# Hybrid attention and MoE step: the sums over values ahead of the turning back and of the second head's transposes

## What is computed

```
z = rmsnorm(x, g1) @ W_in                        # q, k, v of both mixers
s = q @ k.T * d**-0.5 (+ bias);  s = where(valid, s, -1e30)
p = softmax(s)  (mixer A: with a sink in the sum)
o = p @ v                                        # per head
x = x + concat(rmsnorm(oA), rmsnorm(oB)) @ W_out
x = x + sum over 2 chosen experts of w_e * (silu(h Wg) * (h Wu)) @ Wd,   h = rmsnorm(x, g2)
```

## Time and profile before

| | |
|---|---|
| runs before | 1029.91, 1031.77, 1031.78 us; median 1031.77 |
| profiled execution | 1031.24 us, span 1029.3 us, mean granted clock 0.982 |
| TensorE (PE) busy | 956.7 us, 93% of the span |
| VectorE (DVE) busy | 407.1 us, 40% |
| ScalarE (ACT) busy | 306.4 us, 30% |
| attention loop | about 303 to 671 us |
| the 16 DMA engines | about 0.9 busy in most slices behind the loop |

### The profile page before, as it was taken

One profiled execution on the slowest core, in us unless ns is written; L12 is line 12 of the kernel. 1 busy time (PEld: TensorE's weight loads), 2 busy tenths in 40 slices (PEclk: granted clock), 3 DMA queues, 4 the chain that ended last, 5 costly groups with the idle time before them and its releaser, 6 DMA issues. The chain is left out here.

```text
span 1029.3 us, 16232 instructions
## 1 busy us (share of the span) xinstructions
PE 956.7 (93%) x6079; PEld 489.7 (48%) x6079; DVE 407.1 (40%) x1246; ACT 306.4 (30%) x921; POOL 89.2 (9%) x72
## 2 busy tenths in 40 slices
PE   6999999999988989989898998898999999998995
PEld 3444554545365454555555565568444333333331
DVE  0342333422467465665746556575331111101110
ACT  1221222212346354554636445411111111111110
POOL 1000000000030000000000000001222222212111
PEclk9999999999989989999999989999999999999998
DMA  9500111001263011010101041188299999999972
GB/s 357 210 33 9 41 41 41 17 24 41 91 236 130 18 45 62 1 62 1 63 1 62 28 158 62 42 361 334 91 346 382 375 379 393 391 388 391 375 273 41
DMA packets 34441, 164.65 MB, mean 160 GB/s; under 512 B 7809, under 2 KB 9889, under 8 KB 20929
## 3 DMA queue, kind: packets, MB, share of 16 engines
q1 hardware_dynamic: 24192, 134.92, 33.0%
q0 software_dynamic: 6912, 17.32, 6.8%
q10 hardware_dynamic: 3264, 11.44, 2.8%
HBM read 147.10 MB, written 24.41 MB: 167 GB/s over the span
## 5 line engine op out<-in xcount | busy, mean ns | idle before, releaser
L1325 PE MATMUL ps<-arena 128*128 128x512 f32 (+1 forms) x640 | 251.2, 552 | 9.0 <-DMA arena<-in_w_in 9.0
L1325 PEld LDWEIGHTS ps<-arena 128*128 128x128 f32 x640 | 121.0, 190 | 134.1 <-issue 128.8
L1630 PE MATMUL ps<-arena 128*32 128x512 f32 x1536 | 173.8, 603 | 7.4 <-DMA arena<-in_wexp 6.6
L774 ACT ACTIVATE arena<-arena 128x256 f32<-128x256 f32 (+6 forms) x144 | 83.9, 583 | 129.5 <-DVE arena L1071 129.4
L1523 PE MATMUL ps<-arena 128*128 128x512 f32 x224 | 106.0, 605 | 0.0
L1630 PEld LDWEIGHTS ps<-arena 128*32 128x32 f32 x1536 | 51.5, 111 | 111.8 <-issue 107.9
L1067 DVE CUSTOM_DVE_ANT_0 arena<-ps,arena 128x256 f32<-128x256 f32 (+6 forms) x144 | 78.1, 542 | 31.8 <-PE ps L1412 31.5
L1648 PE MATMUL ps<-arena 128*32 128x512 f32 x768 | 87.3, 592 | 0.6 <-ACT arena L878 0.6
L1261 DVE SCALAR_TENSOR_TENSOR arena<-ps,arena 128x256 f32<-128x256 f32 x24 | 11.6, 484 | 167.4 <-ACT arena L870 167.4
L1427 PE MATMUL ps<-arena 128*128 128x128 f32 (+1 forms) x400 | 72.5, 286 | 5.5 <-ACT arena L760 1.7
L979 DVE COPY arena<-ps 128x128 f32<-128x128 f32 (+2 forms) x144 | 52.9, 367 | 48.2 <-PE ps L1427 47.6
(11 more groups left out here) (173 smaller groups left out, 912.9 us busy)
## 6 DMA issues: line engine op xcount, KB each, us to landing
arena<-in_wexp SPq DMA_DIRECT2D x96, 1024.0 KB, 17.4
arena<-in_x SPq DMA_DIRECT2D x18, 512.0 KB, 4.4
arena<-in_w_in ACTq DMA_DIRECT2D x3, 2048.0 KB, 22.7
arena<-in_xT SPq DMA_DIRECT2D x9, 512.0 KB, 3.6
arena<-in_w_out SPq DMA_DIRECT2D x1, 4096.0 KB, 14.0
out_y<-arena SPq DMA_DIRECT2D x8, 512.0 KB, 2.6
h_rows<-arena SPq DMA_DIRECT2D x8, 512.0 KB, 2.9
arena<-in_bias SPq DMA_DIRECT2D x1, 2560.0 KB, 9.0
```

The lines of the kernel that those rows point to most:

```text
L774: nc.scalar.activation(sp[:, u % 4, 0:width], sp[:, u % 4, 0:width], ACT.Exp, bias=shift, accum_out=psum_e[:, t % 2, c:c + 1]).then_inc(s_ ...
L1325: ins = mm(bank(Z_BANK[c], 0, CHUNK[c]), xt[:, j, k, :], w_in[:, a:a + CHUNK[c]], start=(k == 0), stop=(k == KD - 1))
L1630: ins = mm(bank(s % 2)[u:u + UNIT], xgt[:, s % 2, k, u:u + UNIT], ring[expert_of(s, q) % RING][:, k * 512:(k + 1) * 512], start=(k == 0), ...
```

## The change

One line is moved in TensorE's stream: `values(v - 2)` stands behind `scores(v + 1)` and its piece, ahead of `pair_back(v - 3)` and of the second turn.

```diff
                 transpose_probs(2 * v - 2)
                 scores(v + 1)
                 pieces(pe_pieces, 2 * v)
+                values(v - 2)
                 pair_back(v - 3)
                 transpose_probs(2 * v - 1)
                 pieces(pe_pieces, 2 * v + 1)
-                values(v - 2)
                 if 1 <= v < FIRST_OUT:
                     keep_busy(5 - v // 4, 6)
```

## The result

The change is slower: 1055.59 us (four runs, 1054.85 to 1060.29) against 1031.78 (1029.91 to 1032.11), a ratio of 1.0244 with a 95% interval of 1.0212 to 1.0276. The forecast was 1052, in a range of 1040 to 1067. The profiled execution took 1054.85 us, the shortest of the four, with a span of 1053.0.

What follows compares the result with a forecast made beforehand. The prediction took a ring of waits between TensorE, VectorE and ScalarE to bound the attention loop. Five-key tiles 8.8, narrower tiles 6.3, first rounds 2.5 and clock 2.4 made 20.0 us, 1051.2 over 1031.24, said as 1052; range 1040 to 1067.

Steps and rivals of the forecast that it cites:

- The first rival: At the turning back's wait for L740: the moved sums fill the 15.8 us and the kernel is faster, 1022 us; chance 0.06.
- The second: Rival over the whole kernel: TensorE is 93% busy with the same work, so order is indifferent, 1031 to 1033 us; chance 0.05.
- The lost cover: Behind the second turn: without the sums TensorE idles 0.79 us until the result's copies are made and the next first turn starts.
- The sums on the ring: Between L740 and the next second turn: the sums, 0.59 us narrow or 1.25 wide, now lengthen the three engines' circle of waits.
- Steps 1 to 2 and 2 to 3: Second turn to second turn in a five-key tile: 4.92 and 5.88 us, idle growing by 0.41 and 0.51 us.
- step 7 to 0: From round 7's second turn to round 0's in a five-key tile: no idle time before, 0.79 us now.
- 3 to 7: The steps of rounds 3 to 7 in a five-key tile: -0.17, +0.34, +0.33 and 0, together +0.50 us idle, ends 0 and 2.4.
- the sign of being right: In the profile after, a full tile takes 48 to 49 us, and the wait for L740 moves from L1457 to L1444.
- The narrower tiles: The 3.5 tiles with fewer than five keys: 1.8 us lost each, 6.3 us in all, each between 0.8 and 2.2.
- the first rounds: Rounds 2 to 11, with dummy matmuls behind the second turn: the ring grows in about five of ten, 2.5 us, ends 0 and 5.
- The clock: In the loop: added idle time brings four more, half-length stretches at half clock, 0.6 us each, 2.4 us in all.
- The third rival: The clock falls in every tile: 22 us in place of 2.4, 1072 us, or 1062 with one place per tile; chance 0.14.

Runs made afterwards that it cites:

- the dummies: Three dummy matmuls behind the second turn in rounds 1 and 7 from round 12 on: 1055.78 us in the changed kernel, 1038.46 us in the kernel before.
- the sums behind the turn: Kernel before with the sums moved right behind the second turn, ahead of the odd piece, in all rounds: 1028.25 us, run again 1029.58 us.
- Rounds 1 and 7 alone: Kernel before with the sums moved ahead of the turning back only in rounds 1 and 7 of each tile: 1041.61 us, ratio 1.0077.
- the filled waits: Dummy matmuls behind the scores of rounds 2, 3 and 5: 1025.21 us with the sums right behind the second turn, 1048.58 us in the changed kernel.

## Why the prediction was right

**What bounds the kernel**: right. The sums could not fill the wait for L740, since they wait for the same count; L1444 took over L1457's 15.8 us as 17.9. The first rival falls with it. The second (TensorE is full) falls with the time, 24 us more for the same work; the dummies that cost nothing in the changed kernel show the room that came, and in the kernel before, where they cost 6 to 7 us, there was none at that place. One reading was too wide: of the 4.07 us idle in a full tile not all is at waits for the ring. In the tile from 494.40 to 540.84 the trace puts 1.11 and 0.90 us to L740, but 0.73, 0.55 and 0.28 to pieces that wait for L806, L1047 and L1030; the 0.55 is what the sums behind the turn fill.

**The lost cover**: right in size. 1.10 us from second turn to first turn was forecast from the earlier trace rows, 1.11 measured, with 0.73 idle for the 0.79 forecast. Rounds 1 and 7 alone show it by itself. No run has the sums on the ring with the cover kept, so how the loss divides between the two parts is read from the timelines and not from an experiment.

**The sums on the ring**: right, and too small. Steps 1 to 2 and 2 to 3 were forecast at 4.92 and 5.88 us and took 5.08 (503.31 to 508.39) and 6.03 (508.39 to 514.42). Two terms were mis-sized. The turning back ahead of the second turn was taken as 0.11 us from the earlier trace rows; behind the sums it is 0.16 to 0.17 (508.23 to 508.39). And what stands ahead of the sums was taken as it was ahead of the turning back: from L740 to the sums 0.40 us pass (507.23 to 507.63) and not 0.31, and the piece of round 3 takes 0.59 (512.41 to 513.00) and not 0.49. From second turn to second turn, with 0.66 us taken off or put on for the sums that moved, idle time of a five-key tile grew by 0.92 us in step 7 to 0 (0.79 forecast), 0.57 in 1 to 2 (0.41), 0.67 in 2 to 3 (0.51) and 0.77 in 3 to 7 (0.50). So the tile lost 2.93 us instead of 2.2, and took 49.37 us where 48 to 49 was the sign of being right.

**The narrower tiles and the first rounds**: from the turning back of round 2 to that of the next the tile of rounds 18 to 25 grew from 43.71 to 45.89 us and the next from 45.01 to 47.14, 2.1 to 2.2 for the 1.8 taken; these tiles hold stretches at half clock in one kernel or the other. The first rounds, up to the turning back of round 10, went from 19.40 to 20.71 us: 1.3, not the 2.5 forecast, probably because where a round waited less than the sums take, only a part was new. From the turning back of round 10 to the last one the loop grew by 20.7 us, for 17.5 forecast (8.8 + 6.3 + 2.4). The tiles were taken too low and the first rounds too high, so that the sum is nearer than its parts; that much is luck.

**The clock**: 2.4 us forecast; in the profiled executions 3.4 us more lie at half clock, which is worth at most 1.7, and over all four runs the granted clock lacks about 3 us more than the 0.982 of before (0.980 on the mean). The third rival, that each tile falls, did not come about (its smaller figure, by its own terms, is 1061 and not 1062): the changed kernel has four stretches in the loop past the first rounds where the kernel before has three. On the rule of the Trainium skill weighed there ("TensorE: Matmul & The Clock Gate", Part 1), that activity releases the lower clock, the filled waits agree: 20.5 us at half clock became 3.3 when matmuls stood in them.

**Behind the loop**: nothing comes back, as said; 1.45 us more were lost there in the profiled execution, not traced further.

## What to carry to other kernels

In a ring of in-order engines, look at what stands behind the instruction that hands work over (here the second turn): independent work belongs there, since it covers the answer, and the same work ahead of it lengthens the ring. Moving work in front of a wait fills it only if the moved work doesn't wait for the same semaphore count. Part by part, idle time per round is the unit to reckon in; the work itself cancels. But what one instruction takes from start to start depends on what stands behind it, here 0.5 or 0.6 us for the same piece, and such tenths made the forecast of the tile a quarter too low.

## What the runs showed that I had not expected

Dummy matmuls in waits of 0.5 to 1.2 us, off the ring, are worth 4 to 8 us of 1030: in the two profiled executions they left no stretch at half clock (granted clock 0.50, 1.2 GHz) in the loop, where some 17 to 20 us had been. The spread of the runs did not become smaller (3.3 us with them, 2.6 without, five runs each). The order with the sums between the turning back and the turn had 41.1 us at half clock, 17 more than the change, though its waits look alike; that stays open. A second buffer for the sums, which would have let them run ahead of L740, was not tried: it would have to lie in bank 7, where TensorE would write while ScalarE reads, and the other banks are taken. The Trainium skill, "PSUM — Partial Sum Buffer", section "PSUM bank collisions raise a hardware error", says that two engines on one bank and the same partitions at once raise an error; no run here shows it. So what the wait for L740 alone costs the change stays unmeasured.
